# Tiles of the PE array for a hybrid encoder step on one Trainium2 core

## The reference

```python
# sparse attention: scores of an indexer pick keys; a query of the sample sees its stream's
# 128 cached keys and the 16 new ones
score = einsum('bqhs,bqh->bqs', relu(einsum('bqhd,bsd->bqhs', qi, ki)), wi)
logits = where(selected(score), einsum(q, k) / 8, NEG_INF); out = softmax(logits) @ v
# Mamba-2 mixer; each stream of the sample brings a state S (32 heads, 64 x 128)
S_new = S * decay + einsum(B, decay_to_end, x * dt)
y = y_diag + einsum(C, S, exp(a_cum))
h = LN1(alpha * x + (gates * branches) @ w_out)
# PEER: 8 heads pick 16 of 16384 experts per row; u, v are (16384, 1024)
act = gelu(einsum('td,thkd->thk', h, u[expert]))
y = LN2(alpha * h + einsum('thk,thkd->td', gate * act, v[expert]))
```

## Time and profile before

| | |
|---|---|
| median of 3 runs | 2170.71 us (2166.14 to 2176.21) |
| the profiled execution | 2180.12 us |
| its span, first to last instruction | 2177.9 us |
| mean granted clock of TensorE | 0.902 |
| PE busy | 1729.4 us (79% of the span) |
| DVE busy | 1079.5 us (50%) |
| POOL busy | 825.2 us (38%) |
| ACT busy | 415.9 us (19%) |
| moved by DMA | 563.41 MB, mean 259 GB/s |

### The profile page before, as it was taken

One profiled execution on the slowest core, in us unless ns is written; L12 is line 12 of the kernel. 1 busy time (PEld: TensorE's weight loads), 2 busy tenths in 40 slices (PEclk: granted clock), 3 DMA queues, 4 the chain that ended last, 5 costly groups with the idle time before them and its releaser, 6 DMA issues.

```text
span 2177.9 us, 16149 instructions
## 1 busy us (share of the span) xinstructions
PE 1729.4 (79%) x5473; PEld 903.2 (41%) x5473; DVE 1079.5 (50%) x2563; ACT 415.9 (19%) x989; POOL 825.2 (38%) x776
## 2 busy tenths in 40 slices
PE   6979899887986898789898998676577677775676
PEld 5658566433433454544444444222232233232232
DVE  3445465412286873662212445966757535544343
ACT  0121211111113271332211212120101100101101
POOL 0000000000034661331110335677777667767673
PEclk9989999998999999889999999988888878888898
DMA  8712354766477784446564677999999999999996
GB/s 266 268 59 97 126 147 124 244 232 240 155 280 280 246 284 157 154 159 247 174 224 162 212 262 277 331 346 370 326 369 351 365 359 367 370 369 370 357 370 252
DMA packets 223361, 563.41 MB, mean 259 GB/s; under 512 B 20000, under 2 KB 73440, under 8 KB 222848
## 3 DMA queue, kind: packets, MB, share of 16 engines
q0 software_dynamic: 110736, 402.88, 50.4%
q1 hardware_dynamic: 112552, 159.63, 21.6%
HBM read 550.23 MB, written 12.23 MB: 258 GB/s over the span
## 4 chain that ended last, share of the span: by engine, by line
PE 51%; DVE 13%; POOL 13%; issue 8%; DMA 8%; ACT 4%; another core or an unknown queue 2%; SPq 1%; DVEq 0%; POOLq 0%; ACTq 0%
PE bank L783 19%; POOL BIG L643 13%; PE bank L697 7%; PE bank L698 7%; PE bank L745 4%; ACT BIG L1172 3%; DMA wbuf<-in_w_in_dram 3%; PE bank L767 3%; DVE BIG L1521 2%; DMA BIG<-in_peer_v_dram,BIG 2%; PE bank L1091 2%; DVE BIG L2048 1%; DMA BIG<-in_peer_u_dram,BIG 1%; PE bank L1035 1%
## 5 line engine op out<-in xcount | busy, mean ns | idle before, releaser
L643 POOL DMA_INDIRECT BIG<-in_peer_u_dram,BIG x384 | 420.3, 1095 | 1085.5 <-DVEq L2016 614.4
L697 PE MATMUL bank<-BIG 128*128 128x512 f32 x768 | 449.1, 669 | 280.6 <-ACT BIG L1172 175.2
L643 POOL DMA_INDIRECT BIG<-in_peer_v_dram,BIG x384 | 402.0, 1047 | 244.2 <-PE bank L698 103.9
L783 PE MATMUL bank<-wbuf,BIG 128*128 128x512 f32 x1056 | 466.9, 601 | 16.1 <-DMA wbuf<-in_w_in_dram 9.3
L2048 DVE CUSTOM_DVE_ANT_0 BIG<-BIG 128x1024 f32<-128x1024 f32 x256 | 311.3, 1225 | 313.6 <-DMA BIG<-in_peer_u_dram,BIG 278.3
L698 PE MATMUL bank<-BIG 128*128 128x512 f32 x768 | 424.3, 636 | 0.0
L697 PEld LDWEIGHTS bank<-BIG 128*128 128x128 f32 x768 | 156.6, 213 | 498.2 <-issue 472.9
L783 PEld LDWEIGHTS bank<-wbuf,BIG 128*128 128x128 f32 x1056 | 202.2, 193 | 273.8 <-issue 249.8
L698 PEld LDWEIGHTS bank<-BIG 128*128 128x128 f32 x768 | 160.7, 209 | 213.4 <-issue 213.4
L1172 ACT ACTIVATE BIG<-bank 128x512 f32<-128x512 f32 (+5 forms) x225 | 108.9, 515 | 488.5 <-PE bank L783 203.5
L1172 ACT ACTIVATE BIG<-cst,small 128x128 f32<-128x128 f32 x384 | 122.5, 390 | 310.2 <-DVE small L1516 246.1
(11 more groups left out here) (170 smaller groups left out, 1235.2 us busy)
## 6 DMA issues: line engine op xcount, KB each, us to landing
wbuf<-in_w_in_dram SPq DMA_DIRECT2D x24, 2048.0 KB, 8.1
wbuf<-in_w_in_dram SPq DMA_DIRECT2D x16, 1536.0 KB, 7.2
wbuf<-in_w_ssm_br_dram SPq DMA_DIRECT2D x8, 2048.0 KB, 8.1
wbuf<-in_peer_wq_dram SPq DMA_DIRECT2D x8, 2048.0 KB, 8.6
BIG<-in_state_ssm_dram SPq DMA_DIRECT2D x16, 512.0 KB, 5.4
wbuf<-in_w_attn_br_dram SPq DMA_DIRECT2D x4, 2048.0 KB, 8.6
out_s_ssm_dram<-BIG SPq DMA_DIRECT2D x16, 512.0 KB, 3.7
wbuf<-in_w_out_dram SPq DMA_DIRECT2D x4, 2048.0 KB, 7.9
```

Source lines behind the costliest of these rows:

```text
L643: pool.indirect_dma_start(slot, None, table, bass.IndirectOffsetOnAxis(ap=eidx[:, col:col + 1], axis=0)).then_inc(done, 16)
L697: mm(acc[t][0][:, :], dg[:, j, :], slots[j][:, 0:512], start=False, stop=False, skip_group_check=True)
L783: last = mm(dst[:, :], lhs(b, k, toks[t]), wbuf[b][:, k, :], start=(k == 0), stop=(k == KC - 1))
```

## The change

It has four parts. The masks and copies: CTm and Bm are kept for even and odd streams alone (2 in place of 8), the masked queries once in place of four times. The sample's matmuls: `dot_keys` writes one quarter of the partitions (32) with each of four matmuls; `times_values` takes the two halves in turn (the prompt's too); the scan's L1035 becomes four matmuls over 32 rows each with 256 columns, into four banks, and DVE takes a bank for every two streams; L1046 becomes 2 x 4 matmuls, each for one quarter of the partitions. `expert_rows` cuts a rank's product into four matmuls of 64 rows by 64 columns of the diagonal by 512, the two halves of the rows into different banks; `finish` reads the sums with four operations in place of two. The last stage's loop on PE is written out in Python. The table of constants is smaller.

```diff
-    parts["blkcol"] = np.broadcast_to(np.arange(DEC_B)[:, None] == stream[None, :], (P, DEC_B, P))
...
+    odd = stream % 2
+    parts["par"] = odd[:, None] == np.arange(2)[None, :]
+    parts["parcol"] = np.broadcast_to(np.arange(2)[:, None] == odd[None, :], (P, 2, P))
+    parts["pair"] = (t // 64)[:, None] == odd[None, :]
...
-            ssd_v = n + n * G * 4 + G * sum(t > 0 for t in q.tiles) + G * sum(t < 2 for t in q.tiles) + 32 * s
+            ssd_v = n + n * G * 4 + G * sum(t > 0 for t in q.tiles) + G * sum(t < 2 for t in q.tiles) + 64 * s
...
             def expert_rows(t, dg, used, j, slots, landed):
 
-                landed.take(pe) if isinstance(landed, Count) else pe.wait_ge(*landed)
-                mm(acc[t][0][:, :], dg[:, j, :], slots[j][:, 0:512], start=False, stop=False, skip_group_check=True)
-                mm(acc[t][1][:, :], dg[:, j, :], slots[j][:, 512:1024], start=False, stop=False,
-                   skip_group_check=True).then_inc(used, 1)
+                pe.wait_ge(*landed)
+                for i in range(2):
+                    rows = slice(64 * i, 64 * i + 64)
+                    for half in range(2):
+                        last = mm(acc[t][i][64 * half:64 * half + 64, :], dg[rows, j, rows],
+                                  slots[j][rows, 512 * half:512 * half + 512], start=False, stop=False, skip_group_check=True)
+                last.then_inc(used, 1)
...
                                 for j in range(4):
-                                    mm(dst[:, o:o + P], q.qm[:, r, j, :], q.kcT[:, v, j, :], start=(j == 0), stop=(j == 3))
+                                    rows = slice(32 * j, 32 * j + 32)
+                                    mm(dst[rows, o:o + P], q.qm[:, r, rows], q.kcT[:, v, j, :], start=True, stop=True)
...
+                        for k in range(2):
+                            mm(o[k], q.qkv[:, 0, vs], q.PT[:, 1, k::2, :], start=True, stop=False, skip_group_check=True)
+                        for b in range(DEC_B):
+                            for k in range(2):
+                                ob = o[k].rearrange("p (r t) -> p r t", r=2)[:, :, b * DEC_S:(b + 1) * DEC_S]
+                                last = mm(ob, q.vc[:, b, v * HD:(v + 1) * HD], q.PT[:, 0, k::2, b * DEC_S:(b + 1) * DEC_S],
                                           start=False, stop=(b == DEC_B - 1), skip_group_check=True)
...
-                                for half in range(2):
+                                for i in range(4):
                                     dst = vbank()
-                                    vf.give(mm(dst[:, :], q.xdtd[:, c * P:(c + 1) * P], q.Bm[:, 4 * half:4 * half + 4, :],
+                                    rows = slice(32 * i, 32 * i + 32)
+                                    vf.give(mm(dst[:, 0:2 * P], q.xdtd[rows, c * P:(c + 1) * P], q.Bm[rows, :, :],
                                                start=True, stop=True))
...
-                                for b in range(DEC_B):
-                                    last = mm(dst[:, :], q.CTm[:, b, :], q.pT[:, b, :], start=(b == 0), stop=(b == DEC_B - 1))
+                                for k in range(2):
+                                    for j in range(4):
+                                        rows = slice(32 * j, 32 * j + 32)
+                                        last = mm(dst[rows, :], q.CTm[:, k, rows], q.pT[:, 2 * j + k, :],
+                                                  start=(k == 0), stop=(k == 1), skip_group_check=True)
...
-            for t in range(2):
-                if t == 1:
+            for n in range(2 * TURNS):
+                t = n // TURNS
+                if n == TURNS:
                     pe.wait_ge(acc_read, 1)
-                open_sums(t)
-                with loop(pe, TURNS, (dg, 1), *((c, 1) for c in landed)):
-                    dg.take(pe)
-                    for j in range(PB):
-                        expert_rows(t, diag8, v8_used, j, vslot8, landed[j])
-                close_sums(t)
+                if n % TURNS == 0:
+                    open_sums(t)
+                pe.wait_ge(diag_ready, BLOCKS + n + 1)
+                for j in range(PB):
+                    done = n + 1 + (P // SLOTS if slot_sem[j] < SLOTS else 0)
+                    expert_rows(t, diag8, v8_used, j, vslot8, (v_in[slot_sem[j]], 16 * done))
+                if n % TURNS == TURNS - 1:
+                    close_sums(t)
...
-                    own(stt(hv[:, c], hv[:, c], ALPHA, acc[t][n][:, :], ALU.mult, ALU.add))
+                    for i in range(2):
+                        rows = slice(64 * i, 64 * i + 64)
+                        own(stt(hv[rows, c], hv[rows, c], ALPHA, acc[t][i][64 * n:64 * n + 64, :], ALU.mult, ALU.add))
...
-                        for r in range(REP):
-                            last = tt(q.qm[:, r, :, :], bc(v[:, r, :].unsqueeze(1), [4, P]), pair, ALU.mult)
-                        vd.give(last)
+                        vd.give(tt(q.qm, v, bc(pair.unsqueeze(1), [REP, P]), ALU.mult))
...
-                            own(tt(q.CTm, bc(q.xc[:, 20 + g, :].unsqueeze(1), [DEC_B, P]), blkcol, ALU.mult))
-                            own(tt(q.Bm, bc(q.xbt[:, DI + g * P:DI + (g + 1) * P].unsqueeze(1), [DEC_B, P]),
-                                   bc(blk.unsqueeze(2), [DEC_B, P]), ALU.mult))
+                            own(tt(q.CTm, bc(q.xc[:, 20 + g, :].unsqueeze(1), [2, P]), parcol, ALU.mult))
+                            own(tt(q.Bm, bc(q.xbt[:, DI + g * P:DI + (g + 1) * P].unsqueeze(1), [2, P]),
+                                   bc(par.unsqueeze(2), [2, P]), ALU.mult))
...
                                 for half in range(2):
-                                    src = bank()
-                                    for b in range(4):
-                                        bb = 4 * half + b
-                                        sv = q.sst[c % STATES][:, bb, :]
-                                        last = stt(sv, sv, dec[:, c, bb:bb + 1], src[:, b * P:(b + 1) * P], ALU.mult, ALU.add)
-                                    own(last, vd)
+                                    for i in range(2):
+                                        src = bank()
+                                        for b in range(2):
+                                            bb = 4 * half + 2 * i + b
+                                            sv = q.sst[c % STATES][:, bb, :]
+                                            last = stt(sv, sv, dec[:, c, bb:bb + 1], src[:, b * P:(b + 1) * P], ALU.mult, ALU.add)
+                                        own(last, vd)
```

More of the change, by code:

```diff
@@ L296, in lay @@
             if q.streams:
-                q.qm = take(2048).rearrange("p (r j t) -> p r j t", r=REP, j=4)
+                q.qm = take(512).rearrange("p (r t) -> p r t", r=REP)
             top = max(top, big[0])
@@ L934, in times_values @@
                     dst = sbank()
-                    for par in range(2):
-                        o = dst[64 * par:64 * par + 64, 0:256]
-                        vs = slice(O_V + v * HD, O_V + (v + 1) * HD)
-                        if t < 2:
-                            for half in range(t + 1):
-                                last = mm(o, q.qkv[:, half, vs], q.PT[:, half, par::2, :],
-                                          start=(half == 0), stop=(half == t))
-                        else:
-                            mm(o, q.qkv[:, 0, vs], q.PT[:, 1, par::2, :], start=True, stop=False, skip_group_check=True)
-                            for b in range(DEC_B):
-                                ob = o.rearrange("p (r t) -> p r t", r=2)[:, :, b * DEC_S:(b + 1) * DEC_S]
-                                last = mm(ob, q.vc[:, b, v * HD:(v + 1) * HD], q.PT[:, 0, par::2, b * DEC_S:(b + 1) * DEC_S],
+                    vs = slice(O_V + v * HD, O_V + (v + 1) * HD)
+                    o = [dst[64 * half:64 * half + 64, 0:256] for half in range(2)]
+                    if t < 2:
+                        for half in range(t + 1):
+                            for k in range(2):
+                                last = mm(o[k], q.qkv[:, half, vs], q.PT[:, half, k::2, :],
+                                          start=(half == 0), stop=(half == t), skip_group_check=True)
+                    else:
+                        for k in range(2):
[4 more added lines that the diff above has]
+                                last = mm(ob, q.vc[:, b, v * HD:(v + 1) * HD], q.PT[:, 0, k::2, b * DEC_S:(b + 1) * DEC_S],
                                           start=False, stop=(b == DEC_B - 1), skip_group_check=True)
```

15 lines of the change are left out of this document (4 added, 11 removed).

## The result

The changed kernel takes 2091.01 us (median of 4 runs, 2088.24 to 2092.66) beside 2171.64 us (4 runs, 2166.14 to 2176.21) of the kernel before on the same chip: a ratio of 0.963 [0.960, 0.965], or -80.6 us. The forecast was 2072 us, -99; the range, 2040 to 2145, holds the result. The profiled execution took 2088.24 us, its span is 2086.4 us, against 2180.12 and 2177.9 before.

The account below looks back on a forecast made before the run. PE was taken as mostly the bound up to about 1345 us, the gathers after. Terms -1 - 23 - 31 - 35 - 4 - 5 = -99, from the median 2170.7 to 2072 us; range 2040 to 2145.

Parts of the forecast that it names:

- Do tiles overlap?: Tiled matmuls, expert_rows and L1035 above all: full overlap, four pieces in the time of one, 0.16 us per form change.
- The sample's attention: keep_q multiplies once, dot_keys in four column tiles, times_values in turns: -3.5, -16 and -3.5, together -23 us.
- the sample's scan: L1035 and L1046 in tiles, smaller masks: chunk period 6.04 to 5.1 us, L1046 7.03 to 2.0; -31 us taken.
- Constants: Constants and masks at the start: table smaller by 0.59 MB, in a stretch that waits for weights; -1 us.
- The end: Last turn to the close: PE's faster ranks give -6, DVE's longer finish +1.3; together -5 us.
- The prompt's mixer: 34 expert_rows ticks there, each 1.4 us shorter; 47 us on the chain, three quarters taken: -35 us.
- The rival that hands the mixer's gain to the gathers and DVE: Prompt's mixer gives -12 in place of -35, last stage and end together -5; 2099 us, chance 0.11.
- The last stage: Bound by gathers; eight ranks go from 13.7 to about 7 us in a 22.7 us turn: -4, bounds 0 and -25.
- The rival of late code: PE's written-out last stage arrives late, 21 more code packets each stopping PE 6 us: 2198 us; slower, chance 0.04.
- The clock: Last stage: TensorE granted 0.85; if at 1.2 GHz throughout with less work, eight ranks take 13.7 us, as now.
- The base: -99 was reckoned against the profiled 2180.12 us, 9.4 over the median, then applied to the median 2170.7.
- the rival of the row tiles: Row tiles do not overlap, only two column tiles run at a time: gains left 29, 2142 us, chance 0.16.

Follow-up runs that it names:

- the copy of the change: The changed kernel run once more, unaltered, as reference for the kernels beside it: 2092.78 us, ratio 0.963 to the kernel before.
- the kernel with the ticks alone: Kernel before, with expert_rows cut in 64x64 tiles only for the sample's ranks run in the prompt's mixer: 2158.39 us, ratio 0.990.
- the kernel with one of them: Changed kernel with the last stage's rank products on the whole array again, ticks still tiled, loop still written out: 2087.59 us, ratio 0.962.
- the last kernel: Changed kernel with half of each row gathered in the last stage and dots there and in the ticks over 512 columns: 2066.29 us, ratio 0.949.

## Why the prediction was right, and where its sizes were off

**Do tiles overlap?** Right, and it carried the case: four tiles at once, in `expert_rows` and in L1040 (0.71 us with its modelled end, 0.64 to the fill behind it). The prediction took four pieces in the time of one; the tick, 1.88 us, is 1.72 and one change of form. The Trainium skill's 3.07x (TensorE: Matmul & The Clock Gate, Part 3) doesn't hold for these tiles of 64 rows: in the last stage's turns one four starts 0.43 us behind the other (1920.63, 1921.06, 1921.49 in the copy of the change), as one MATMUL of 512 columns did, which is the full 4x. The 15 us that the prediction would have added by that figure lead to 2087 us, near the 2091 measured, but only by luck: the ticks don't hold those 15 us. The Trainium skill's rule that a change of mode drains TensorE (TensorEngine Tiling (Array Packing), Key Properties) agrees, at 0.16 us a change, measured twice now.

**The sample's attention** (-23, measured -21.8) and **the sample's scan** (-31, measured -31.9) were right, by the steps as put: chunk 5.17 us (5.1 said), sums 1.85 us (2.0), the mixer up to the prompt's qkv shorter by 55.2 (54). **Constants** -1.2 (-1), which no trace can tell: that stretch ends at 112.6 to 118.3 us in the kernels with the smaller table. **The end** -5.3 from the last turn's start (-5).

**The prompt's mixer** was the term that was mis-sized: -35 taken, 28.3 us in the profiled pair (4.0 + 4.0 - 0.3 + 16.0 + 4.8, rounded), 19.5 in the kernel with the ticks alone. The shortfall is in the attention: 14 ticks a stretch, 1.56 us each, are 22 us, and 4.0 came in this pair. Over all traces it is less: 139.5 to 141.2 us in the four kernels with ticks on the whole array, 136.2 to 141.3 in the seven with tiled ticks and all their gathers and dots. The groups of PE by line, 713 to 853 us before, then 654 to 790 us after:

```profile
L697 PE MATMUL bank<-BIG 128*128 128x512 f32 x56 | 32.7, 667 | 9.8 <-DMA BIG<-in_peer_v_dram,BIG 9.2 <-ACT BIG L1172 0.6
L698 PE MATMUL bank<-BIG 128*128 128x512 f32 x57 | 30.8, 623 | 0.0
...
L908 PE MATMUL bank<-BIG 64*128 64x128 f32 (+1 forms) x80 | 15.7, 337 | 2.6 <-DVE BIG L1665 1.9 <-issue 0.8
L897 PE MATMUL bank<-cst,BIG 128*64 128x128 f32 x80 | 10.9, 279 | 0.0
```

```profile
L698 PE MATMUL bank<-BIG 64*64 64x512 f32 x224 | 36.2, 744 | 13.9 <-DMA BIG<-in_peer_v_dram,BIG 9.1 <-ACT BIG L1181 3.3 <-issue 1.3
...
L909 PE MATMUL bank<-BIG 64*128 64x128 f32 (+1 forms) x80 | 18.9, 387 | 5.1 <-DVE BIG L1676 5.1
L898 PE MATMUL bank<-cst,BIG 128*64 128x128 f32 x80 | 12.6, 309 | 0.0
```

Whole busy times give the sum (the ticks' own 63.5 us count overlapping modelled ends twice). PE was busy 124.4 of 140.2 us and is busy 111.5 of 136.0: 12.9 us less, of the 22. So unchanged work and the ticks themselves run slower by 9 us: the granted clock of this stretch fell from 0.96 to 0.87, L909 takes 18.9 us where it took 15.7, L898 12.6 for 10.9. That goes with the tiles: in this stretch the clock is 0.84 to 0.90 in the nine kernels with tiled ticks, 0.95 to 0.99 in the four with the whole array and the one with column tiles alone. And PE idles 9 us more, 24.5 us for 15.8: 13.9 us ahead of the ticks (was 9.8) and 5.1 ahead of the dots (was 2.6).

Of the wait ahead of the ticks, the gathers of v hold 9.1 us, as before (9.2); what came on top is mostly ACT's diagonals (3.3, was 0.6). PE also waits on gathers whose issue takes POOL long beside VectorE's dots. POOL, VectorE and PE in time in the changed kernel:

```profile
721.26 1.09 PE L698 MATMUL bank<-BIG 64*64 64x512 f32 x8
...
721.60 3.61 POOL L641 DMA_INDIRECT BIG<-in_peer_v_dram,BIG  x1 [0.30 <-issue]
722.04 1.21 DVE L1532 CUSTOM_DVE_ANT_0 BIG<-BIG 128x1024 f32<-128x1024 f32 x1
723.18 1.21 DVE L1532 CUSTOM_DVE_ANT_0 BIG<-BIG 128x1024 f32<-128x1024 f32 x1
723.39 1.09 PE L698 MATMUL bank<-BIG 64*64 64x512 f32 x8 [1.04 <-DMA BIG<-in_peer_v_dram,BIG]
724.53 0.69 DVE L1754 TENSOR_TENSOR BIG<-BIG,small 128x512 f32<-128x512 f32 x1
```

Such long issues came with the shorter ticks: seven of 30 are over 2 us here, two were before. They stand in this trace's chain (POOL 24.8% of the stretch), but they don't decide, as the kernel with one of them shows: there ACT and VectorE stand in the chain, at 138.6 us. So in the attention several chains are about as long as PE's, and which one takes how much stays open. The prediction named "DVE's dots" and "the gathers of v" as next and took a quarter off; in the attention it was four fifths. The rival that hands the mixer's gain to the gathers and DVE (-12) had the right size for this stretch, not for the products, which gave 16.0 us.

**The last stage**: -4 taken, 0 measured (3.9 in the profiled pair is luck: the copy of the change took 723.6 us and the whole array 716.2). The reason given, the bytes, is right for the changed kernel but thinner than it was put: POOL's issuing stands right behind. The rival of late code named gaps called "issue" on PE within a turn as its sign, and they are there. The written-out order alone has none, but its turn is half as many MATMULs. The packets of code speak against the rival: 56, were 36, so 20 more where the prediction said 21, each about 1 us long and one every 45 us in the last stage, and 8 of the 17 turns with gaps have none beside them. The queues from 1927.8 to 1946 us, a turn of 18.2 us with five gaps of more than 1.3 us; q8, the queue that grew with PE's code, isn't among them:

```profile
q0 software_dynamic: 1945, 7.08, 100.6%
q14 instruction: 1, 0.01, 0.1%
```

The gaps cost the last stage little, since the gathers take 22.7 us a turn. They appear with tiles, of columns alone too, and a written-out order together; tiles in the old loop weren't tried, and what holds these MATMULs stays open.

**The clock**: the prediction said that at 1.2 GHz throughout eight ranks would take no longer than before. It sat at 0.68 of the full one, at no cost that the total shows in that stage; that it would cost in the mixer too was missed.

**The base**: -99 was set against a profiled execution 9.4 us above its median and carried over to the median. By profiles the gain is 91.9 us (2180.12 - 2088.24), by medians 80.6. So of the 18 us between -99 and -80.6 about 7 are the terms, and the rest is that the profiled execution before was a long one and that after the shortest of its four.

**Slips in the sums**: a rank of u and v is 1.05 MB, so 256 of them at 367 GB/s are 731 us and not 714; the gains left by the rival of the row tiles add up to 30, not 29. Neither moves the forecast.

## What to carry to other kernels

Diagonal or block-masked products on the whole array can be cut into four tiles (here 64 x 64, 128 x 32 and 32 x 128): the same work in four pieces took the time of one, and 0.16 us went for each change of form, so group the tiles of one form. Before counting PE time as gained, look at what PE's longer work had covered: here the chains of POOL, ACT and VectorE in the attention, and a granted clock that was lower where PE was less busy (0.87 at 82%, 0.96 at 89%). Where one resource is at 97%, halve it alone before planning on the gain: here POOL's issuing stood within 2% of it, and with that relieved too the last stage still took 716 us.

## What was not expected of the hardware

- A gather's issue on POOL takes 0.94 us, but up to 2.0 us beside one or two dots of VectorE, 3.6 us beside a copy, two dots and a `TENSOR_TENSOR`. The Trainium skill (SBUF — State Buffer, Who interferes with whom) says that a VectorE instruction with two inputs in SBUF holds out a GpSimd instruction that reads SBUF, while it infers that `tensor_tensor` doesn't hold up the making of descriptors. By the first rule the trace agrees; the inference doesn't hold for these gathers, whose indices lie in SBUF (an issue beside a lone `TENSOR_TENSOR` of 1.22 us took 1.62 us in the last kernel).
- Four MATMULs on four tiles start 7 ns apart, and the next four 0.43 to 0.48 us after them.
- In about half of the last stage's turns some tiled MATMULs of the last three ranks start 0.7 to 2.8 us apart, with nothing named that they wait for.
- In the last stage PE was granted 0.68 at a busy share of 57%; with the whole array there in the same kernel, 0.84 at 70%.
